# Moving six expert-weight chunks one place back in the load order of a hybrid layer's first stages

## The reference

```
xn   = rmsnorm(x)
proj = xn @ w_in                        # 1024 -> 3584: xc, gB, gC, q, k, v, g
a    = gB * conv3_causal(gC * xc)       # 4 channel groups of 128
r    = silu(g) * groupnorm(retention(rotary(q), rotary(k), v))   # 4 heads of 128
x    = x + concat([a, r]) @ w_out
logits = rmsnorm(x) @ w_router + b_router       # 32 experts, top 4, softmax gates
x    = x + sum over the chosen experts of  gate * (swiglu(xn @ w_up[e] + b_up[e]) @ w_down[e] + b_down[e])
y    = rmsnorm(x)
```

## Time and profile before

| | |
|---|---|
| time of the runs | median 1088.58 us of 3 (1085.95 to 1090.34) |
| the profiled execution's own time | 1085.15 us |
| its span, first to last instruction | 1083.2 us |
| TensorE busy | 1065.2 us, 98% of the span |
| mean granted TensorE clock | 0.999 of full speed |
| read from HBM | 427.00 MB, 397 GB/s over the span |

### The profile page before, as it was taken

One profiled execution on the slowest core, in us unless ns is written; L12 is line 12 of the kernel. 1 busy time (PEld: TensorE's weight loads), 2 busy tenths in 40 slices (PEclk: granted clock), 3 DMA queues, 4 the chain that ended last, 5 costly groups with the idle time before them and its releaser, 6 DMA issues.

```text
span 1083.2 us, 13193 instructions
## 1 busy us (share of the span) xinstructions
PE 1065.2 (98%) x5692; PEld 446.5 (41%) x5693; DVE 361.7 (33%) x572; ACT 152.6 (14%) x302; POOL 11.9 (1%) x28
## 2 busy tenths in 40 slices
PE   9999999999999999999999999999999999999997
PEld 7888664333333333333333333333333333333332
DVE  3376534233332223333322222323332232232234
ACT  2121144101111110111111111011111101011113
POOL 1000010000000000000000000000000000000002
PEclk9999999999999999999999999999999999999999
DMA  8975949999999999999999999999999999999994
GB/s 292 312 276 198 407 161 381 412 428 426 433 434 427 433 431 430 431 429 431 433 429 428 434 431 428 430 432 431 429 430 434 430 429 430 426 427 427 430 415 177
DMA packets 40907, 431.47 MB, mean 398 GB/s; under 512 B 4456, under 2 KB 19852, under 8 KB 25104
## 3 DMA queue, kind: packets, MB, share of 16 engines
q1 hardware_dynamic: 40240, 430.41, 94.8%
q10 hardware_dynamic: 608, 0.20, 0.1%
HBM read 427.00 MB, written 3.48 MB: 397 GB/s over the span
## 4 chain that ended last, share of the span: by engine, by line
PE 83%; DMA 15%; SPq 1%; issue 0%; ACT 0%; DVE 0%; ACTq 0%; POOLq 0%; DVEq 0%; POOL 0%
PE bank L1015 37%; PE bank L1034 15%; DMA ring_all<-in_w_up 14%; PE bank L695 8%; PE bank L1079 6%; PE bank L989 4%; PE bank L1026 2%; PE bank L805 2%; PE bank L997 2%; PE bank L1007 1%; PE bank L1072 1%; PE bank L1091 1%; PE bank L813 1%; DMA ring_all<-in_w_in 1%; SPq L516 1%; PE bank L648 1%
## 5 line engine op out<-in xcount | busy, mean ns | idle before, releaser
L1015 PE MATMUL bank<-ring_all,work 128*64 128x512 f32 x2048 | 484.6, 600 | 7.7 <-DMA ring_all<-in_w_up 7.7
L1015 PEld LDWEIGHTS bank<-ring_all,work 128*64 128x64 f32 x2048 | 134.7, 136 | 257.4 <-issue 247.9
L1034 PE MATMUL bank<-ring_all,work 128*64 128x512 f32 x992 | 225.3, 596 | 0.0
L1847 DVE TENSOR_TENSOR h_tok<-h_tok,bank 128x1024 f32<-128x1024 f32 (+1 forms) x67 | 81.8, 1221 | 236.6 <-PE bank L1079 230.7
L1034 PEld LDWEIGHTS bank<-ring_all,work 128*64 128x64 f32 x992 | 68.4, 137 | 129.1 <-issue 128.2
L695 PE MATMUL bank<-work,ring_all 128*128 128x264 f32 x384 | 87.0, 387 | 1.0 <-DMA ring_all<-in_w_in 1.0
L1817 DVE TENSOR_TENSOR work<-bank,bias_up 128x1024 f32<-128x1024 f32 x32 | 39.2, 1224 | 124.0 <-PE bank L1026 124.0
L695 PEld LDWEIGHTS bank<-work,ring_all 128*128 128x128 f32 x384 | 72.5, 190 | 13.4 <-DMA ring_all<-in_w_in 1.4
L1079 PE MATMUL bank<-work 64*128 64x512 f32 (+1 forms) x268 | 75.1, 637 | 0.0
L1834 DVE TENSOR_TENSOR work<-work 128x512 f32<-128x512 f32 x32 | 22.2, 693 | 108.8 <-ACT work L1419 108.8
L1403 ACT ACTIVATE work<-bank 128x264 f32<-128x264 f32 x32 | 12.5, 390 | 315.9 <-PE bank L1007 315.9
(11 more groups left out here) (236 smaller groups left out, 549.0 us busy)
## 6 DMA issues: line engine op xcount, KB each, us to landing
ring_all<-in_w_up SPq DMA_DIRECT2D x48, 4096.0 KB, 32.8
ring_all<-in_w_down SPq DMA_DIRECT2D x24, 4096.0 KB, 33.9
ring_all<-in_w_up SPq DMA_DIRECT2D x30, 2048.0 KB, 38.1
ring_all<-in_w_down SPq DMA_DIRECT2D x13, 2048.0 KB, 40.5
ring_all<-in_w_in SPq DMA_DIRECT2D x13, 1024.0 KB, 5.1
ring_all<-in_w_down SPq DMA_DIRECT2D x6, 1024.0 KB, 21.8
ring_all<-in_w_out SPq DMA_DIRECT2D x4, 1024.0 KB, 11.7
ring_all<-in_w_up SPq DMA_DIRECT2D x4, 1024.0 KB, 6.1
```

The costliest lines, as they stand in the source:

```text
L1015: mm = pe.matmul(bank[half * CAP:(half + 1) * CAP, up_bank(n) + b, :].rearrange("q (k p) -> q p k", k=KT), x, src[:, half * FF + b * 512:h ...
L1034: mm = pe.matmul(bank[half * CAP:(half + 1) * CAP, Y, :], av[:, 2 * i + k, :], src[:, k * D + half * 512:k * D + (half + 1) * 512], start= ...
L1847: tt(rows, rows, bank[0:m, b:b + 2, :], ALU.add).then_inc(comb_added, 1)
```

## The change

The six chunks of the loop move from j = 3, 5, ..., 13 to j = 5, 7, ..., 15. `w_router` moves with the first of them to j = 5. The last one, with its wait for `summed`, now comes behind the second piece of `w_out` and ahead of `store_states`. The two loads of `b_up` and the store of the convolution row go from j = 3 to behind `b_router`, ahead of the wait for `hs_copied`.

```diff
-                    if j >= 3:
-                        k = (j - 3) // 2
-                        if j == 13:
+                    if j >= 5:
+                        k = (j - 5) // 2
+                        if j == 15:
                             sp.wait_ge(summed, 5)
-                        elif j == 15:
-                            store_states(sp)
                         if j % 2 and k < FIRST - 1:
                             sp.dma_start(ring_a[:, k, :], chunk_src(stream[k])).then_inc(landed[k], 16)
-                        if j == 3:
+                        if j == 5:
                             sp.dma_start(w_rt[:], w_router[0].rearrange("(k p) e -> p k e", p=P)).then_inc(misc_in, 16)
-                            for half, p0 in enumerate(BU):
-                                sp.dma_start(x_tok[p0:p0 + E, 2, :], b_up[0, :, half * FF:(half + 1) * FF]).then_inc(bu_in, 16)
-                            sp.dma_start(conv_sample[0, :, 0, :], state_conv[0, :, 1, :]).then_inc(out_done, 16)
+                        if j == 15:
+                            store_states(sp)
                         if j == 17:
                             sp.wait_ge(state_out, 16)
...
                 sp.dma_start(b_rt[:], b_router.partition_broadcast(P)[:, 0, :]).then_inc(b_rt_in, 16)
+                for half, p0 in enumerate(BU):
+                    sp.dma_start(x_tok[p0:p0 + E, 2, :], b_up[0, :, half * FF:(half + 1) * FF]).then_inc(bu_in, 16)
+                sp.dma_start(conv_sample[0, :, 0, :], state_conv[0, :, 1, :]).then_inc(out_done, 16)
                 sp.wait_ge(hs_copied, 4)
```

## The result

Over 14 runs each, the changed kernel takes 1091.14 us (1089.46 to 1093.3) where the kernel before takes 1088.99 (1085.95 to 1092.27). The ratio is 1.0028, 95% interval 1.0018 to 1.0039: 3.0 us more (2.0 to 4.3), inside the 0.5%. The ratio is the one put on record with its interval; the two medians alone give 1.0020, 2.2 us. Forecast were 4.2 us more. The profiled execution took 1090.95 us, 5.8 more than the one profiled of before. That the profiles differ by 5.8 us and the runs by 3.0 turns out to be the most useful clue.

What follows compares the result with a forecast made beforehand. The prediction took the kernel as bound by TensorE until the stream starts and by the DMA engines at the end. Its terms, -0.97 + 5.2 = +4.2 us on a median of 1088.58, gave 1092.8 us, range 1087.2 to 1096.8.

Steps and rivals of the forecast that it cites:

- What bounds the kernel: Whole kernel: TensorE binds until the stream starts, DMA engines at the end; a TensorE delay ahead of 150 us reaches the end.
- Part 1: At j = 3, near 39.2 us: `w_in` chunk 4 is issued sooner and TensorE's wait for it goes; gain 0.97 us.
- the whole wait of 0.97 us goes, and no more than it can: TensorE's wait for `w_in` chunk 4 at 39.2 us: the gain is all of it, 0.97 us, and at most that.
- Part 2: From 107 us to `w_out` 2: one more expert chunk ahead makes TensorE wait 5.2 us (bounds 4.6 and 5.5).
- the term of 5.5 us for 2 MB: Queue ahead of `w_out` 2: the added chunk delays its landing by 5.5 us, against 0.3 us of room.
- the lower bound of 4.9: Queue ahead of `w_out` 2: the least cost of 2 MB, 4.9 us, at the stream's 429 GB/s.
- The rival of the clock: Behind the new `w_out` wait: TensorE's clock falls, +3.7 us (+1.9 to +5.6), net 7.9, 1096.5 us, slower by over 0.5%; 26%.
- Part 3: End of the first stages: later landings and the moved `w_router`, `b_up` and row loads or stores stay hidden, at nothing.
- the lower bound of 1.1: SP's issues of `b_up` twice and the row, behind `b_router`: as little as three times 0.35 us.
- the 7.27: How long, in us, `b_up` twice and the row held SP at j = 3 behind a full queue.
- The sum: Whole kernel: -0.97 + 5.2 = +4.2 us, within 0.5%, on the slow side.

Runs made afterwards that it cites:

- chunk5_late: The changed kernel with the last of the six chunks moved from ahead of the states to behind `w_out` 3; 1084.64 us, ratio 0.995 to the kernel before.
- two_ahead: The changed kernel with the chunks one more place back, so three chunks stand between 107 us and `w_out` 2; 1101.86 us, ratio 1.0122 to the kernel before.
- warm18: The changed kernel with 18 matmuls into an unused bank ahead of the wait for `w_out` 2; 1090.35 us, ratio 1.0013 to the kernel before.
- before_filler: The kernel before with 22 filler matmuls ahead of the wait for `w_out` 2, no load moved; 1096.84 us, ratio 1.0074 to the kernel before.
- late2: The changed kernel with the last two of the six chunks behind `w_out` 3; 1084.78 us, ratio 0.9951 to the kernel before.
- chunks_only: The changed kernel with `w_router`, `b_up` and the row kept at j = 3, so only the chunks move; 1091.76 us, ratio 1.0018 to the kernel before.
- warm: The changed kernel with 36 matmuls into an unused bank ahead of the wait for `w_out` 2; 1093.08 us, ratio 1.003 to the kernel before.
- bup_only: The kernel before with only the `b_up` loads and the convolution row's store moved behind `b_router`; 1086.4 us, ratio 0.9967 to the kernel before.
- before_look3: The kernel before, unchanged, profiled again in search of a slower execution; that execution took 1091.66 us.

## Why the prediction came out as it did

It was right on the total and on the waits that go and come. Both of its parts were sized too small, a gain and a loss, and that the total still came near is luck.

**What bounds the kernel.** Right. A shift of TensorE ahead of 150 us reaches the end in full: own time less start of the experts is 918.0 (before), 918.8 (after), 919.7 (chunk5_late), 919.1 (two_ahead), and 918.3 to 919.9 in all others but warm18 (921.6), over a spread of starts of 17 us. That scatter of 1.9 us, 3.6 with warm18, lies behind the start of the experts. The earlier trace rows are not all waits of the kernel before: 1.2 us for VectorE and two short ones of 0.6 us together stand beside them, and the first is the same after.

**Part 1: mechanism right, mis-sized: 0.97 us priced, 3.6 to 5.4 measured.** `w_in` 4 was issued at 32.52 and landed 5.0 us later, at 37.5, as forecast, and the wait is gone. The ratios are 0.9967 for `b_up` and the row alone and 0.995 for all of the change but the late chunk (chunk5_late). The step that failed is "the whole wait of 0.97 us goes, and no more than it can". The wait in the one execution profiled was taken for the wait of the kernel. It is 1.0, 1.0, 1.2 and 3.3 us in four executions of the kernel before and 1.8 us in before_filler, and the longest is followed by 2.9 us of half speed. The table of times said so beforehand: a median 3.4 us above the profiled execution, which I carried along as an offset instead of asking where it lay. That most slower runs of before are slow for this reason is argued from one such profile, from the mean clock of the runs (0.995 to 0.997 in most of those over 1089, 0.998 or 0.999 in all of chunk5_late's) and from the scatter that goes in chunk5_late and late2 with the wait.

**Part 2: mechanism right, the term of 5.5 us for 2 MB too large, and the clock left out of the sum.** `w_out` 2 landed at 135.6. With everything 0.85 us sooner (the issue at 106.17 against 107.02) it would have landed at 131.9 - 0.85 = 131.1 without the chunk, so the chunk cost 4.6 us, just under the lower bound of 4.9; two_ahead gives 5.0 for the second. The wait was 4.2 us and not 5.2. The rival of the clock, at 26%, came true in its mechanism, not in its outcome (over 0.5% slower): 1.7 us in this profile, 3.1 in that of chunks_only, where 3.7 were priced. The rule cited there from the Trainium skill (TensorE: Matmul & The Clock Gate, Why this matters for your kernels) agrees with the traces: the clock fell to the 1.2 GHz level during or right behind the waits of 3.3, 4.2, 4.2 and 9.2 us. It doesn't cover all of them, as the last section shows.
The profiles close on Part 2: of the 6.5 us between the starts of the experts in chunk5_late and the changed kernel, 4.2 are the wait, 1.7 the clock, and 0.6 lie ahead of the wait (TensorE reaches it at 131.46 instead of 130.86).

**Part 3** held throughout. `w_router` landed at 51.7, where 52 at most was forecast, ahead of its use at 54.65. `b_up` and the row held SP for 1.7 us (134.30 to 136.00), nearer the lower bound of 1.1 than the 7.27; SP waited for `hs_copied` with 12.8 us to spare. No wait of TensorE for `b_router`, `w_router` or `b_up` appears. The queue was served in order, as the landings had shown.

**The sum again.** Forecast were -0.97 + 5.2 = +4.2. In the profiles, at the start of the experts, it is -1.4 + 6.5 = +5.1. In the runs Part 1 is -5.4 (3.4 to 7.6) by chunk5_late, so that Part 2 must be the rest, +8.4, to give the 3.0 measured; it was not measured by itself, and the medians put it at 6.5 to 7.1. Against the forecast that is a gain 2.6 to 4.4 us larger and a loss 1.3 to 3.2 us larger, and the two errors cancelled in part.

What stays open: how often the kernel before has the long wait for `w_in` 4, seen once in four profiles; why its queue was slower in that one; and what the runs lose in Part 2 beyond the 5.9 us (4.2 + 1.7) of the one profile. The 3.1 us of low clock in chunks_only would make 7.3 of it.

## What to carry to other kernels

Before a load is moved, write down for each load behind it in the queue when it lands and when it is first used: one here had 0.3 us of room, and the same 2 MB that cost 6 us ahead of it cost nothing behind the loads with a deadline. A wait of TensorE has two prices, its own length and the slow matmuls behind it (0 behind 1 us here, 1.5 to 3.1 us behind 3.3 to 9.2). And when the median of the runs lies several microseconds over the profiled execution, get more profiles before anything is priced, for a small wait in one may be the short end of a long one; here only the fourth showed it.

## What the runs showed of the hardware beyond that

The clock doesn't fall behind waits alone, nor behind each one. In warm the granted clock was at 0.50 from 172 to 175 us with TensorE busy throughout, after a stretch of many small matmuls. In bup_only it was at 0.50 from 891.5 to 894.5 us, behind a wait of 2.35 us for `w_up` that ended at 890.70 (16 matmuls took 5.35 us there, 3.65 elsewhere), while a wait of 2.4 us for `w_up` in before_look3 had no such stretch behind it. Each of these stretches came in one execution, and adds a microsecond or two of scatter. Twice the same wait of 4.2 us went with slow stretches of different length (1.7 and 3.1 us lost). In the wait of 9.2 us the clock fell while TensorE still stood, and the eight matmuls behind it took 5.22 us, 1.5 more than usual: the longest wait did not have the highest price behind it.

An issue of SP may be held by what is queued ahead rather than by its own size: the first load of `b_up`, 128 KB, held SP for 5.96 us at j = 3 and both together for 0.89 us at 134.3 us.
